# The gate of the experts' sum, made from its weights in the mixer or between the mixer and the experts

## The reference, cut to what matters

```python
mod = silu(c) @ ada_w + ada_b                      # (6 * 1024,) for each of the two sequences
shift1, scale1, gate1, shift2, scale2, gate2 = split(mod, 6)
h = rmsnorm(x, norm1_g) * (1 + scale1) + shift1
x = x + gate1 * mixer(h)                           # two recurrences, gated attention, w_out
h = rmsnorm(x, norm2_g) * (1 + scale2) + shift2
x = x + gate2 * hier_moe(h)                        # 16 experts, two of them for each token
y = rmsnorm(x, final_g)
```

## Time and profile before

| | us |
|---|---|
| median of 3 runs | 608.67 |
| the profiled execution, its own time | 607.79 |
| its span in the trace | 606.0 |
| TensorE busy | 554.0 (91%) |
| VectorE busy | 298.9 (49%) |
| ScalarE busy | 203.4 (34%) |
| GpSimd busy | 103.2 (17%) |

### The profile page before, as it was taken

How to read it: one execution, slowest core, us unless ns; L and a number is a source line. 1 busy time by engine, 2 the same in 40 slices (tenths; PEclk the granted TensorE clock), 3 DMA queues, 4 the chain that set the end, 5 groups by cost and what they waited for, 6 DMA issues and landing times.

```text
span 606.0 us, 6409 instructions
## 1 busy us (share of the span) xinstructions
PE 554.0 (91%) x2358; PEld 298.3 (49%) x2358; DVE 298.9 (49%) x592; ACT 203.4 (34%) x372; POOL 103.2 (17%) x113
## 2 busy tenths in 40 slices
PE   0899999999999899999999999689999999999970
PEld 0545545554446556566545555464454454454430
DVE  0632547947304764011344455515764666666671
ACT  5322299963312200543411122210000443443440
POOL 3000000001502110000000000040232354453332
PEclk9999999999999999999999999869999999999995
DMA  7986663118528611500019511169999989999311
GB/s 276 387 250 212 187 230 117 36 35 309 195 87 226 243 38 36 192 0 1 1 30 386 209 69 70 70 217 397 392 361 373 344 324 356 342 361 347 147 50 47
DMA packets 74417, 120.44 MB, mean 199 GB/s; under 512 B 13889, under 2 KB 31634, under 8 KB 74386
## 3 DMA queue, kind: packets, MB, share of 16 engines
q1 hardware_dynamic: 63880, 104.23, 49.3%
q0 software_dynamic: 10368, 15.75, 7.3%
q10 hardware_dynamic: 138, 0.04, 0.0%
HBM read 115.51 MB, written 26.51 MB: 234 GB/s over the span
## 4 chain that ended last, share of the span: by engine, by line
PE 58%; DVE 5%; ACT 2%; issue 2%; POOL 0%; POOLq 0%; DVEq 0%
PE ms L1447 18%; PE ps L1380 12%; PE ps L1097 9%; PE ps L1468 8%; PE ps L1430 2%; PE ps L1316 2%; PE ms L1351 1%; PE ps L1306 1%; PE ps L1265 1%; DVE tmp L1768 1%; PE ms L1419 1%; DVE tmp L1738 1%; PE ps L1342 1%; PE ps L1457 1%; PE ps L1285 0%
## 5 line engine op out<-in xcount | busy, mean ns | idle before, releaser
L1097 PE MATMUL ps<-r,wring 128*128 128x512 f32 (+1 forms) x512 | 143.7, 437 | 1.4 <-ACT mixT L893 0.9
L1097 PEld LDWEIGHTS ps<-r,wring 128*128 128x128 f32 x512 | 79.0, 191 | 67.1 <-issue 66.1
L1380 PE MATMUL ps<-wring,mixT 128*128 128x512 f32 x160 | 72.1, 599 | 0.5 <-DVE tmp L1859 0.5
L1447 PE MATMUL ms<-wring,tmp 128*128 128x512 f32 x128 | 57.7, 593 | 1.3 <-DVE tmp L2038 1.3
L680 POOL DMA_INDIRECT mixT<-h_rows,slot_tok x16 | 19.6, 1222 | 194.2 <-DVE slot_tok L1966 180.2
L1380 PEld LDWEIGHTS ps<-wring,mixT 128*128 128x128 f32 x160 | 29.3, 191 | 32.0 <-issue 31.3
L1447 PEld LDWEIGHTS ms<-wring,tmp 128*128 128x128 f32 x128 | 23.6, 190 | 27.8 <-issue 26.3
L1039 ACT ACTIVATE tmp<-ms 128x256 f32<-128x256 f32 x16 | 6.1, 383 | 88.8 <-PE ms L1447 88.8
L1172 PE MATMUL ps<-wring,r 128*128 128x512 f32 x80 | 35.6, 598 | 0.3 <-issue 0.3
L2073 DVE TENSOR_TENSOR tmp<-ps,tmp 128x512 f32<-128x512 f32 x32 | 22.1, 691 | 16.8 <-PE ps L1468 16.8
L1447 PE MATMUL ms<-r,tmp 128*128 128x512 f32 x64 | 30.3, 621 | 0.0
(11 more groups left out here) (318 smaller groups left out, 823.2 us busy)
## 6 DMA issues: line engine op xcount, KB each, us to landing
wring<-in_ada_w_dram SPq DMA_DIRECT2D x12, 2048.0 KB, 12.1
wring<-in_exp_w_dram SPq DMA_DIRECT2D x8, 2048.0 KB, 24.5
wring<-in_w_in_dram SPq DMA_DIRECT2D x16, 512.0 KB, 4.0
r<-in_exp_w_dram SPq DMA_DIRECT2D x4, 2048.0 KB, 22.5
wring<-in_exp_w_dram SPq DMA_DIRECT2D x8, 1024.0 KB, 19.7
tmp<-in_exp_w_dram SPq DMA_DIRECT2D x4, 2048.0 KB, 23.6
wring<-in_w_out_dram SPq DMA_DIRECT2D x2, 2048.0 KB, 12.2
vtok<-in_exp_w_dram SPq DMA_DIRECT2D x4, 1024.0 KB, 17.6
```

Source lines behind the costliest of these rows:

```text
L1097: i = mm(d, lhsT, r, start=first, stop=last)
L1380: i = mm(product(f"mx{t}")[:, half * 512:(half + 1) * 512], mixT[:, k, t * P:(t + 1) * P], w[:, k, :], start=(k == 0), stop=(k == KD - 1))
L1447: i = mm(ms[:, b, :], xgT[:, b, k, :], e13[u % 4][:, k, :], start=(k == 0), stop=(k == KD - 1))
```

## The change

Modulations 10 and 11 leave the mixer. Their `modulation`, `take_mod`, `turn_modulation` and VectorE sums are gone from the hand-written order, and `A2`, `rows_t` and `mod_rows` shrink from eight rows to six. `rows[0][3]` is now loaded with the bias `ada_b` of `gate2`, broadcast from DRAM; `rows[1][3]` isn't loaded.

In their place: `late_modulation(n, ks)` makes the same products behind the last router products, modulation 10 and the first half of 11 ahead of `rank(4)`, the second half of 11 behind `table(4)`. ScalarE copies each result to `late_row[n]` (in `mtmp`). `spread(n)` multiplies a selector `seqs` (in `mask`, made by three small VectorE operations) by that row. This sums the four groups of 32 rows and broadcasts the result to all partitions: one product for sequence 0, one for sequence 1 less sequence 0. VectorE adds the first to the bias (`late_base`), ScalarE copies the second to `rows[1][3]` (`late_diff`). spread(0) stands ahead of the first turned tokens, spread(1) ahead of hidden(1), and `turn_a(0)` and the first gate row wait for all four results.

Piece a10 goes through slot 1 of `wring`, where e13(1) was loaded before, and a11 through slot 0 once the first half of mx4 is done. e13(1) is now loaded after modulation 10 is made, e2(1) after modulation 11.

```diff
-            for name in ("a8", "a9", "a10", "a11"):
+            for name in ("a8", "a9"):
                 load_piece(name)
...
             load13(0)
             load2(0)
-            load13(1)
+            load_piece("a10")
             for t in range(NT):
+                if t == NT - 1:
+                    load_piece("a11")
                 sp.wait_ge(h2_ready, t + 1)
...
             wait_taken(sp, "mx4")
+            sp.wait_ge(late_made, 1)
+            load13(1)
             sp.wait_ge(gx_in[0], 16)
+            sp.wait_ge(late_made, 2)
             load2(1)
             load13(2)
...
+            act.wait_ge(late_made, 1)
+            A(late_row[0], ps[:, 1, 0:512], ACT.Copy).then_inc(late_taken, 1)
             act.wait_ge(gready, 1)
...
+            act.wait_ge(late_made, 2)
+            A(late_row[1], ps[:, 1, 512:D], ACT.Copy).then_inc(late_taken, 1)
...
+            take_diff(0)
             silu_of(0)
+            take_diff(1)
...
             values(3)
-            two_of(modulation, 10)
             values(4)
-            two_of(turn_modulation, 10)
...
+            def late_modulation(n, ks):
+                wait_piece(pe, f"a{10 + n}")
+                w = weights(f"a{10 + n}")
+                for k in ks:
+                    r = 32 * (k % 4)
+                    i = mm(ps[r:r + 32, 1, 512 * n:512 * n + 512], cs[:, k, :], w[:, k, :], start=(k < 4), stop=(k >= 4),
+                           skip_group_check=True)
+                if ks[-1] == KD - 1:
+                    i.then_inc(late_made, 1)
+
+            def spread(n):
+                pe.wait_ge(seqs_ready, 1)
+                pe.wait_ge(late_taken, n + 1)
+                for s in range(2):
+                    i = mm(ps[:, 2 - n, 512 * s:512 * s + 512], seqs[:, s, :], late_row[n], start=True, stop=True)
+                i.then_inc(late_rows, 1)
+
+            wait_taken(pe, f"mx{NT - 1}")
+            wait_taken(pe, f"hh{NT - 1}")
+            late_modulation(0, range(KD))
+            late_modulation(1, range(0, KD // 2))
             rank(NT - 1)
             table(NT - 1)
+            late_modulation(1, range(KD // 2, KD))
             pe.wait_ge(gates_placed, 1)
...
+            spread(0)
             turn_x(0)
             hidden(0, range(KD))
             turn_x(1)
+            spread(1)
...
+            dve.wait_ge(att_ready, HEADS)
+            link(V.tensor_reduce(lam[:, 0, 0:2], ident[:, :].rearrange("p (r n) -> p n r", n=32)[:, 0:2, :], AX.X, ALU.add))
+            link(tt_(lam[:, 0, 1:2], lam[:, 0, 1:2], lam[:, 0, 0:1], ALU.subtract))
+            V.tensor_copy(seqs[:, :, :], lam[:, 0, 0:2].rearrange("p (s a) -> p s a", a=1).to_broadcast([P, 2, P])) \
+                .then_inc(seqs_ready, 1)
...
-            link(tt_(rows[1][3], rows[1][3], rows[0][3], ALU.subtract))
+            for n in range(2):
+                cols = slice(512 * n, 512 * n + 512)
+                dve.wait_ge(late_rows, n + 1)
+                tt_(rows[0][3][:, cols], ps[:, 2 - n, 0:512], rows[0][3][:, cols], ALU.add).then_inc(late_base, 1)
```

More of the change, by code:

```diff
@@ L262, in hybrid_step @@
         n_head = len(order)
-        modulations = [2, 3, 0, 1, "x"] + list(range(4, 12))
+        modulations = [2, 3, 0, 1, "x"] + list(range(4, 10))
         def gates_order(ch):
@@ L279, in hybrid_step @@
         order += [("v0", "A")] + turned(6, 7) + [("v1", "A")] + adaln(8, 9)
[L280 removed]
+        order += [("v2", "A")] + turned(8, 9) + [("v3", "A"), ("v4", "A")]
         for g in range(4):
@@ L483, in load_piece @@
                 n = passing[i].index(name)
-                if n:
+                if name == "a10":
+                    sp.wait_ge(product_ready, made["yl3"])
+                elif name == "a11":
+                    sp.wait_ge(mx_half, NT)
+                elif n:
                     sp.wait_ge(product_ready, made[last_use[passing[i][n - 1]]])
@@ L547, in load_row @@
             def load_row(seq, kind):
-                i = 4 * seq + kind
+                i = 3 * seq + kind
                 sp.dma_start(rows[seq][kind], rows_d[i * D:(i + 1) * D].rearrange("(a n) -> a n", a=1).to_broadcast([P, D])) \
@@ L552, in _ @@
             wait_taken(sp, "kvB3")
-            for kind in range(4):
+            for kind in range(3):
                 load_row(0, kind)
+            sp.dma_start(rows[0][3], ada_b[0:1, 5 * D:6 * D].to_broadcast([P, D])).then_inc(rows_in[0], 16)
             for s in range(2):
```

55 lines of the change are left out of this document (33 added, 22 removed).

## The result

The changed kernel took 605.49 us (median of 11 runs, 604.68 to 608.53), the kernel before 609.5 in the same comparison (11 runs): a ratio of 0.9945, 95% interval 0.993 to 0.9961. The forecast was 606.3. Run once more beside the experiments, it took 606.87 (8 runs) against 608.85 (25 runs): 0.9954, interval 0.9932 to 0.9975. Over all 19 runs its median is 606.38.

A forecast was written before the change was run, and what follows sets the result against it. TensorE bounds the mixer and the experts from the first turned tokens, VectorE the stretch between; -4.2 + 0 + 0.2 + 1.2 + 0.4 = -2.4 us gives 606.3 us on the median, range 603.6 to 608.4.

The forecast's parts named there:

- The removal: At the values, taking modulations 10 and 11 and their transposes off TensorE's unbroken queue gains 3.57 + 0.66 = 4.2 us.
- 1.4 forecast: Before og0, TensorE's wait for the tile load grows from 0.44 to about 1.4 us.
- no wait at the next carry: After og0, the 0.66 us stall for VectorE's carry of the state goes.
- wrong if the mixer is shorter by less than 3.5 us: Sign in the mixer: a gain under 3.5 us there would show the forecast wrong.
- The late half: Between mixer and experts: late products 0 before rank(4), +0.2 us behind table(4), spreads +1.2 and +0.4 us.
- both spreads: Ahead of turned tokens, spread(0) adds +1.2 us (0.7 to 1.7); ahead of hidden(1), spread(1) adds +0.4 us.
- I take half clock: Behind table(4), modulation 11's second half takes 1.8 us at half clock against 0.9 at full: +0.2 us.
- Nothing for the loads: Moved weight pieces and gathers cost nothing: the 11th piece lands 2.9 us early, and a late gather hides behind spread(0).
- rival three: At hidden(1), e13(1) arrives late: 29 us makes the kernel 0.2% slower, 31 us gives 611.9; chance 0.08 with another case.
- The selector's three operations: On VectorE ahead of the router's terms, some 0.8 us, covered by a 2.74 us wait: cost nothing.
- Rival one: Between mixer and experts, late products fill the holes and the clock never falls: 601.9 to 606.4 us, middle 604.2; chance 0.17.
- Rival two: Before rank(4), the clock falls on the late products, delaying rank(4) 1.0 us: 607.4 to 609.0, middle 608.2; chance 0.15.

The follow-up runs named there:

- no_late: The changed kernel without modulations 10 and 11, the spreads and their waits, e13(1) loaded early as before: 604.7 us, 0.9942 to the kernel before.
- first execution: One profiled run of the unaltered changed kernel, from the group with mean clock 0.981: 606.38 us, span 604.6.
- second execution of after: Another profiled run of the unaltered changed kernel, from the slower group with mean clock 0.976: 608.07 us, span 606.3.
- fill_before: The kernel before plus twelve unused products, shaped like the late ones, in the hole before rank(4): 608.1 us, 1.0003 to the kernel before.
- og_fill: The changed kernel plus six unused products in the wait before og0: 605.67 us, 0.9952 to the kernel before.
- e13_behind: The changed kernel with e13(1) queued behind gather(0) in place of ahead of it: 608.79 us, 0.999 to the kernel before.
- spread_first: The changed kernel with spread(0) ahead of the gates' sum, measured twice: 605.24 us (0.9929 to the kernel before) and 603.85 us (0.9922).
- split_e13: spread_first with half of e13(1) moved behind gather(0): 606.22 us, 0.996 to the kernel before.
- narrow_spread: The changed kernel with both spreads 8 columns wide in place of 512: 606.7 us, 0.9958 to the kernel before.
- split_fill: split_e13 plus six unused products in the wait before og0: 607.19 us, 0.9951 to the kernel before.
- og_fill_spread: The changed kernel with both six unused products before og0 and spread(0) ahead of the gates' sum: 604.82 us, 0.9941 to the kernel before.
- early_og: The changed kernel with the og tiles loaded early into another slot: 609.98 us, 0.9997 to the kernel before.

## Why the prediction was right, point by point

**The removal, -4.2 us: right.** no_late shows it at the place (4.28 at the first mix product), at rank(4) (4.2) and in medians (4.1). The chain behind it was right as well: 1.53 us before og0 against 1.4 forecast, and no wait at the next carry.

**What hid at og0: missed.** I counted the longer wait as a wait alone. In the first execution the clock fell in it, 1.43 us. That, and a start 1.28 us later in code that the change doesn't touch (the first modulation took 3.43 us in place of 2.42, and its data came 0.27 later), is why rank(4) stands at 389.50, only 1.57 us earlier, and not at 386.9: 4.28 - 1.43 - 1.28 = 1.57. The sign "wrong if the mixer is shorter by less than 3.5 us" would have misled here: the clock at og0 and the start have to be taken out first. In no_late and in the second execution of after og0 ran at full clock.

**The late half, +1.8 us forecast (0.2 + 1.2 + 0.4): +0.2 in the first execution.** From the router's last products to rank(4) it is 4.33 us after and 4.35 before: the late products cost 0, as forecast. From rank(4) to the gates' sum 3.86 against 4.67: -0.8, where I had +0.2 by assuming half clock for the second four products; fill_before shows the -0.8 alone. From the sum to hidden(1) 18.62 against 17.55: +1.1 for both spreads, where I had +1.6. spread(0) took 3.55 us, all of it at half clock. The clock was back 3.8 us after it began (4.9 in the second execution), where the earlier trace rows gave 3.2. The step that failed is "I take half clock". I had left the fall at 388 to 389, where the kernel before has it, so that rank and table stayed at half as before. In the first execution it came at 394.2, behind all of them. The step wasn't baseless: in og_fill and e13_behind the clock fell at 389.8 and 390.7, and there the second four products took 1.94 us in place of 1.06, as I had priced them. But rank(4) was still at full clock, and from it to the sum it was 4.17 and 4.00 us, still less than 4.67.

**The sum: partly luck.** Without its late start the first execution gives -4.28 + 1.43 + 0.24 = -2.6 us, next to my -2.4. That agreement is luck: the missed 1.43 at og0 and the 1.6 that the late half cost less than forecast cancel. The base was luck in part too. I took 2.4 from a median of 608.67 of three runs, a ratio of 0.9961. Measured were 0.9945 and 0.9954, 3.4 and 2.8 us, and 0.9961 is the very end of the first interval. And the range of 603.6 to 608.4 doesn't follow from its reason: the middles of rivals one and two are 604.2 and 608.2.

**Nothing for the loads: right.** The 11th piece landed after 7.8 us, e13(1) after 12.7 against the 25.4 that I had as available (388.2 to 411.98, 23.8, were there), so rival three was far off. In the first execution the gather took 7.0 us in place of 4.6 and landed at 392.9 + 7.0 = 399.9, 0.9 before the tokens could be turned.
The Trainium skill, "DMA: Bandwidth & Descriptors", section "Issuing engines are not separate DMA queues", says that transfers from different engines share the same 16 DMA engines. The runs agree in part: 7.0 us with e13(1) in flight in the first execution, 4.6 to 5.4 with it behind the gather, but 4.8 to 5.2 with it in flight in the second.

**The selector's three operations: right.** They took 0.6 us (300.07 to 300.66), and VectorE still waited 2.16 us behind them, against 2.74.

**The clock, rivals one and two.** Rival one, no fall at all, appeared in no profile. Rival two did, where I had 0.15: in the second execution rank(4) starts 7.01 us after the router's row in place of 4.35, and the whole is 606.3 against 606.0, the +0.3 at the end of its working. The agreement of the number is luck again, since the terms are others. The fall came at 383.0, with the router's last products and ahead of all late products, so rank(4) lost 2.66 us and not 1.0. The gather took 4.8 us and not 9.3, and the tokens waited for spread(0) at half clock and not for the gather. The six runs of that group have a median of 608.13; I had 608.2. So the single time hid a mixture: 13 of 19 runs at 605.27, below the forecast, and 6 at rival two's time. That all six are rival two is inferred from their clock; one was profiled. None of the nine runs at 604.68 to 605.49 was profiled, so where their clock fell isn't known. The mean of all 19 is 606.35, and the forecast 606.3 is right partly because it lies between the groups.
The Trainium skill, "TensorE: Matmul & The Clock Gate", section "What's actually happening", calls the throttled clock the default that activity releases. The runs agree in the direction (with work in the hole before rank(4) the fall came at 394.2 in the first execution, where it was 388.5 before). In the second it had fallen at 383.0, ahead of this work, and was back at 389.9, near the work's end.

**What stays open** is which execution falls where. The three profiled runs that fell at og0 (the first of after, the first of spread_first, split_e13) all kept the clock until 394 or later. Of those with the late products that had no fall before 380, six of seven (the second of after, narrow_spread, og_fill, split_fill, e13_behind, the second of spread_first) fell at 383 to 390.7, and og_fill_spread at 395.5. early_og, which fell at 213.9 and 299.2, kept it until 394.8. A fall seems to be put off by an earlier one, but nothing here sets it at will, and the first modulation, ahead of all edits, took between 2.36 and 3.64 us from run to run, which moves all that follows.

## What to carry to other kernels

Products that left an unbroken TensorE queue were worth nearly their full time here: 4.3 of 4.5 us, since a short DMA wait took the rest. The same products, put into a hole where TensorE waits for VectorE, cost nothing where they ran at full clock and ended before TensorE was released. Work out what they cost at half clock as well (here 2.7 us), because some runs will have that. Compare profiles of two kernels only where the clock fell at the same places; a span that is 2 us shorter may come from ahead of the edit. Before a load is moved out of the way of a small transfer, look whether its queue is full for the next 100 us: here moving it cost 1.5 to 2.7 us there, more than the earlier gather gave.

## What the hardware showed that was not expected

- A wait of 1.5 us before og0 was enough for the clock to be at half behind it in some executions and not in others of the same kernel (og0 in 6.02 and 4.59 us), and removing the wait moved the fall elsewhere without a gain in time (early_og, og_fill).
- One kernel has groups of executions about 3 us apart (medians 605.27 and 608.13) that its mean clock tells apart (0.981 and 0.976): 0.005 of a span of 605 us is 3.0 us. The kernel before has its own, mostly 607.8 to 610.3 at 0.975 to 0.979, and a few at 611.2 to 611.7 at 0.969 or 0.970.
- Three indirect gathers beside one 2 MB load took 7.0 us to land, 6.3 to 6.6 in the second spread_first, but 4.8 to 5.2 in the second execution of after, where the load had started 3.5 us behind two stores of 512 KB and not 1.0 us. With the load behind the first gather it was 4.6 to 5.4.
